# Column sums of the norms on four 32-column tiles of TensorE

## What is computed

```python
def layer_norm(x, g, b):
    mu = xf.mean(-1, keepdims=True)
    var = jnp.square(xf - mu).mean(-1, keepdims=True)
    y = (xf - mu) * lax.rsqrt(var + LN_EPS) * g + b
...
        h = layer_norm(ALPHA * h + mix, ln_mix_g[layer], ln_mix_b[layer])
        ff = conv_ffn(h, ...)
        h = layer_norm(ALPHA * h + ff, ln_ffn_g[layer], ln_ffn_b[layer])
...
def rms_norm(x, g):
    y = xf * lax.rsqrt(jnp.mean(xf * xf, axis=-1, keepdims=True) + EPS)
    return y * g
```

## Time and profile before

| | us |
|---|---|
| median of 3 runs | 1501.68 (1500.94 to 1501.72) |
| profiled execution | 1501.82 |
| its span in the trace | 1500.0 |
| PE busy | 1463.2 (98%) |
| DVE busy | 865.6 (58%) |
| ACT busy | 610.9 (41%) |
| POOL busy | 493.3 (33%) |

### The profile page before, as it was taken

The page is one execution under the profiler, slowest core; times in us unless marked ns, Lnnn a source line. Parts: engine busy times, 40 slices in busy tenths (PEclk is TensorE's granted clock), DMA queues, the critical chain, the costliest instruction groups (busy, mean ns, idle before and its releaser), DMA issues.

```text
span 1500.0 us, 23770 instructions
## 1 busy us (share of the span) xinstructions
PE 1463.2 (98%) x9390; PEld 1207.8 (81%) x9390; DVE 865.6 (58%) x1262; ACT 610.9 (41%) x768; POOL 493.3 (33%) x368
## 2 busy tenths in 40 slices
PE   6999999999999999999999999999999999999999
PEld 5887887898888888889776988888888897777677
DVE  6787777476655660155686667556620374564741
ACT  3655554362223222236565443232221355655541
POOL 3000000215454544532221245545454524422222
PEclk9999999999999999999999999999999999999999
DMA  7421222502223223232202122232223312311211
GB/s 226 116 86 60 83 74 85 183 27 90 109 84 112 84 100 123 85 112 85 85 29 85 57 82 87 88 108 87 109 85 107 130 57 84 132 69 71 71 57 57
DMA packets 22592, 137.24 MB, mean 91 GB/s; under 512 B 2488, under 2 KB 4840, under 8 KB 7280
## 3 DMA queue, kind: packets, MB, share of 16 engines
q1 hardware_dynamic: 17280, 124.79, 23.5%
q10 hardware_dynamic: 5232, 11.32, 2.9%
HBM read 131.89 MB, written 4.21 MB: 91 GB/s over the span
## 4 chain that ended last, share of the span: by engine, by line
issue 41%; PE 27%; POOL 24%; DVE 3%; ACT 2%; DVEq 1%; DMA 1%; ACTq 0%; POOLq 0%; SPq 0%
POOL WL L448 15%; POOL WL L457 9%; PE pair L484 7%; PE pair L486 7%; PE pair L485 7%; PE pair L1079 1%; PE pair L667 1%; ACT WH L1185 1%; PE pair L1066 1%; DVE WL L1672 1%; PE pair L998 1%; PE pair L696 1%; PE pair L1056 1%; DMA RAW<-stream 1%; PE pair L663 0%
## 5 line engine op out<-in xcount | busy, mean ns | idle before, releaser
L484 PE MATMUL pair<-AH,WH 128*128 128x512 f32 (+1 forms) x1240 | 474.7, 383 | 16.8 <-POOL WL L448 12.1
L448 POOL TENSOR_TENSOR WL<-RAW,WH 128x512 fp32r<-128x512 f32 x236 | 321.8, 1396 | 487.6 <-ACT WH L1185 487.6
L486 PE MATMUL pair<-AH,WL 128*128 128x512 f32 (+1 forms) x1240 | 463.5, 374 | 0.0
L485 PE MATMUL pair<-AL,WH 128*128 128x512 f32 (+1 forms) x1240 | 463.3, 374 | 0.0
L1185 ACT ACTIVATE WH<-RAW 128x2048 fp32r<-128x2048 f32 x107 | 204.7, 1913 | 466.1 <-PE pair L486 453.3
L457 POOL TENSOR_TENSOR WL<-RAW,WH 128x512 fp32r<-128x512 f32 x128 | 171.3, 1369 | 500.4 <-ACT WH L1185 500.4
L484 PEld LDWEIGHTS pair<-AH,WH 128*128 128x128 f32 x1240 | 233.6, 188 | 66.2 <-issue 12.4
L486 PEld LDWEIGHTS pair<-AH,WL 128*128 128x128 f32 x1240 | 233.7, 188 | 42.2
L485 PEld LDWEIGHTS pair<-AL,WH 128*128 128x128 f32 x1240 | 233.9, 189 | 41.1 <-issue 1.9
L2015 DVE TENSOR_SCALAR CA<-pair,PAR 128x512 f32<-128x512 f32 x88 | 67.3, 806 | 146.9 <-PE pair L486 144.0
L484 PE MATMUL pair<-GH,WH 128*128 (+2 forms) x416 | 149.8, 360 | 0.1
(11 more groups left out here) (247 smaller groups left out, 1889.2 us busy)
## 6 DMA issues: line engine op xcount, KB each, us to landing
RAW<-stream SPq DMA_DIRECT2D x115, 1024.0 KB, 4.9
H<-x_t SPq DMA_DIRECT2D x3, 1024.0 KB, 9.6
bias_rows<-ROWS ACTq DMA_DIRECT2D x1, 2048.0 KB, 23.0
BIAS<-bias_rows ACTq DMA_DIRECT2D x1, 2048.0 KB, 7.9
FBC<-forget_rows ACTq DMA_DIRECT2D x4, 512.0 KB, 3.6
out<-H ACTq DMA_DIRECT2D x8, 256.0 KB, 2.0
H<-x_t SPq DMA_DIRECT2D x2, 512.0 KB, 6.9
CON<-consts ACTq DMA_DIRECT2D x1, 513.5 KB, 4.2
```

What stands on the lines that cost most here:

```text
L448: pool.tensor_tensor(WL[w][:, part], RAW[raw][:, part], WH[w][:, part].bitcast(F32), ALU.subtract).then_inc(w_lo, 1)
L484: pe.matmul(out_, wh, xh, start=start, stop=False, skip_group_check=shared)
L485: pe.matmul(out_, wh, xl, start=False, stop=False, skip_group_check=shared)
L486: return pe.matmul(out_, wl, xh, start=False, stop=stop, skip_group_check=shared)
```

## The change

Half B's sums of norms 0 to 2 (`tile_sums` in place of `half_sums`): each of the four operands of a sum goes through a 128 x 32 slice of `con["mean"]` into its own 32 output partitions, so the four matmuls use four column tiles of the array. ACT copies the 128 x 256 result out of PSUM into SY3 or SS2 (`take_sums`, put between `square(1, 3)` and `gain(0, 3)`), and PE multiplies that by the whole `con["mean"]` (`tile_totals`, one matmul each, after place 4 of the first chunk). The result is 1/32 of the mean, and `variance` multiplies by 32. The rms sums of both halves go the same way (`rms_tiles`, `take_rms`, `rms_totals`): two rounds of four tiled matmuls, a copy by ACT, one whole matmul. `half_sums` stays for norm 3. `rms_tiles(1)` runs in the middle of `value(1, 0)` and `rms_totals(1)` behind it; before, all of `rms_sums(1)` stood ahead of it. ACT's and DVE's lists of the last norm are put in another order.

```diff
+            def tile_sums(idx):
+                ts = cols_of(1)
+                first, second = (bk(b)[:, ts] for b in LN_SUMS[idx])
+                p = LN_PAIRS[idx][3]
+                pe.wait_ge(y_ready, 8 * idx + 8)
+                pe.wait_ge(y_added, 2 * idx + 2)
+                for g, y in enumerate((SY3[:, 1, 0], SY3[:, 1, 1], H[:, 2 * p, ts], H[:, 2 * p + 1, ts])):
+                    mm = pe.matmul(first[BLK * g:BLK * g + BLK], con["mean"][:, 0:BLK], y, start=True, stop=True)
+                mm.then_inc(t_summed, 1)
+                pe.wait_ge(y2_added, 2 * idx + 2)
+                pe.wait_ge(y_squared, 8 * idx + 8)
+                for g, y2 in enumerate((SS2[:, 1, 0], SS2[:, 1, 1], SQ2[:, 1, 3, 0], SQ2[:, 1, 3, 1])):
+                    mm = pe.matmul(second[BLK * g:BLK * g + BLK], con["mean"][:, 0:BLK], y2, start=True, stop=True)
+                mm.then_inc(t_summed, 1)
+            def tile_totals(idx):
+                for power, tiles in enumerate((SY3, SS2)):
+                    pe.wait_ge(t_copied, 2 * idx + power + 1)
+                    pe.matmul(bk(LN_SUMS[idx][power])[:, cols_of(1)], con["mean"], tiles[:, 1, 0], start=True, stop=True).then_inc(y_summed, 1)
...
-                half_sums(idx)
+                tile_sums(idx)
...
-                part(c0, 0, range(4, 8))
+                part(c0, 0, (4,))
+                tile_totals(idx)
+                part(c0, 0, (5, 6, 7))
...
-            def rms_sums(half):
+            def rms_tiles(half):
                 ts = cols_of(half)
-                for i, p in enumerate(LN_PAIRS[3]):
-                    pe.wait_ge(h_squared, 4 * half + i + 1)
-                    for c in range(2):
-                        mm = pe.matmul(bk(6 + half)[:, ts], con["mean"], SQ2[:, half, i, c], start=i == 0 and c == 0, stop=i == 3 and c == 1)
-                mm.then_inc(h_summed, 1)
+                for r in range(2):
+                    pe.wait_ge(h_squared, 4 * half + 2 * r + 2)
+                    for g in range(4):
+                        mm = pe.matmul(bk(6 + half)[BLK * g:BLK * g + BLK, ts], con["mean"][:, 0:BLK], SQ2[:, half, 2 * r + g // 2, g % 2],
+                                       start=r == 0, stop=r == 1)
+                mm.then_inc(h_tiled, 1)
+            def rms_totals(half):
+                pe.wait_ge(h_copied, half + 1)
+                pe.matmul(bk(6 + half)[:, cols_of(half)], con["mean"], SQ2[:, half, 0, 0], start=True, stop=True).then_inc(h_summed, 1)
...
-            rms_sums(0)
+            rms_tiles(0)
+            rms_totals(0)
...
-            rms_sums(1)
-            value(1, 0)
+            value(1, 0, mid=lambda: rms_tiles(1))
+            rms_totals(1)
...
+                def take_sums():
+                    for power, tiles in enumerate((SY3, SS2)):
+                        act.wait_ge(t_summed, 2 * idx + power + 1)
+                        act.activation(tiles[:, 1, 0], bk(LN_SUMS[idx][power])[:, cols_of(1)], ACT.Copy).then_inc(t_copied, 1)
+                def take_rms(half):
+                    act.wait_ge(h_tiled, half + 1)
+                    act.activation(SQ2[:, half, 0, 0], bk(6 + half)[:, cols_of(half)], ACT.Copy).then_inc(h_copied, 1)
...
                     last_gain(0, 3)
+                    take_rms(0)
+                    spread(1)
+                    last_spread(0)
                     split_early(c0 + 2)
...
-                    spread(1)
-                    last_spread(0)
-                    last_gain(1, 0)
                     high(0, 0)
                     high(0, 1)
+                    last_gain(1, 0)
+                    split_next(c0 + 1)
                     last_gain(1, 1)
                     last_gain(1, 2)
-                    split_next(c0 + 1)
+                    high(0, 2)
                     last_gain(1, 3)
-                    high(0, 2)
                     high(0, 3)
+                    take_rms(1)
...
+                take_sums()
                 gain(0, 3)
...
-                    dve.tensor_copy(MEAN[:, ts], mean)
+                    if half and idx < 3:
+                        dve.tensor_scalar(MEAN[:, ts], mean, float(BLK), None, ALU.mult)
+                    else:
+                        dve.tensor_copy(MEAN[:, ts], mean)
...
                     centre(1, 1)
+                    scale(1, 1)
                     last_low(0, 0)
-                    scale(1, 1)
                     last_low(0, 1)
                     centre(1, 2)
                     scale(1, 2)
+                    gained(0, 2)
                     centre(1, 3)
                     scale(1, 3)
-                    gained(0, 2)
                     gained(0, 3)
```

More of the change, by code:

```diff
@@ L278, in build @@
         sg_made, pool_w_loaded, sink_put = sem("sg_made"), sem("pool_w_loaded"), sem("sink_put")
+        t_summed, t_copied, h_tiled, h_copied = (sem(n) for n in ("t_summed", "t_copied", "h_tiled", "h_copied"))
         z_abs, z_exp, f_made, f_stored = (sem(n) for n in ("z_abs", "z_exp", "f_made", "f_stored"))
@@ L1023, in gates, with value @@
                 half(E_CHUNK[j], m)
-            def value(part, t):
+            def value(part, t, mid=None):
                 n = N_V + part
@@ L1029, in value @@
                 for k in range(4):
+                    if mid and k == 2:
+                        mid()
                     if t == 0:
@@ L1364, in last_spread @@
                     act.wait_ge(h_summed, half + 1)
-                    rstd(VAR[:, ts], bk(6 + half)[:, ts], 1.0, con["eps_rms"]).then_inc(h_rstd, 1)
+                    rstd(VAR[:, ts], bk(6 + half)[:, ts], float(BLK), con["eps_rms"]).then_inc(h_rstd, 1)
                 def high(half, p):
@@ L1890, in variance @@
                     dve.wait_ge(y_summed, 4 * idx + 2 * half + 2)
-                    dve.tensor_tensor(VAR[:, ts], second, VAR[:, ts], ALU.subtract)
+                    if half and idx < 3:
+                        dve.scalar_tensor_tensor(VAR[:, ts], second, float(BLK), VAR[:, ts], ALU.mult, ALU.subtract)
+                    else:
+                        dve.tensor_tensor(VAR[:, ts], second, VAR[:, ts], ALU.subtract)
                     dve.drain()
```

## The result

The changed kernel takes 1514.02 us (median of 6 runs, 1512.93 to 1515.14) against 1500.79 us (6 runs of the kernel before beside it): ratio 1.0086, 95% interval 1.0075 to 1.0097. It is slower by 13.2 us; 1508.6 was forecast, with 1511.5 as the upper end. The direction was right; about half of the loss was seen coming. The profiled execution took 1512.93 us, its span 1511.1.

What follows compares the result with a forecast made beforehand. PE and half B's chain were taken to end together, so delaying gain(0,3) costs time: norms 0 to 2 +7.3, last norm -0.4, sum +6.9 us on 1501.82, giving a median of 1508.6 us, range 1504.0 to 1511.5.

Steps and rivals of the forecast that it cites:

- What bounds the norms: Norms 0 to 2: PE and half B's chain end together; the chain hangs on gain(0,3), delayed by 2.45 us.
- What the change takes off PE: Sums: 1.64 us less in each of three norms, 2.05 us less twice for the rms sums, together 9.0 us.
- Rival (2): All tiled sums: the tiles run one by one, each norm losing 1.23 us more; 1514 us; chance 5%.
- Norms 0 to 2, +7.3: Half B of three norms: ACT's copies delay gain(0,3), losing 2.45, 2.4 and 2.45 us, in sum +7.3 us.
- Nothing later takes it back: Behind norms 0 to 2: PE has no such idle time and ACT's next weight split moves along; +7.3 us stays.
- The last norm, -0.4: Last norm: of 4.1 us taken off PE, 0.4 us is left after stalls; bounds -2.9 and +1.5.
- The same step, second place: Last norm: last_spread(1), behind copy, VM and the head's inverse root on ACT, comes at 1251.0, not 1250.64.
- The sum: Whole kernel: 7.3 - 0.4 = +6.9 us on 1501.82, so 1508.7; as a median 1508.6 us.
- The range: Whole kernel: 1504.0 to 1511.5 us, meant to hold 8 in 10.
- Rivals (1): Whole kernel: PE's saved time reaches the end, the rms halves giving 4.1 us; 1497.7 us; chance 6%.
- Rival (3): Whole kernel: the delay is real but half is made up by slack or shorter stalls; 1503 us; chance 7%.

Runs made afterwards that it cites:

- e3: The changed kernel with only take_sums moved behind gain(0,3) on ScalarE: 1509.63 us.
- e6: The kernel before with only the last norm's new order of ScalarE and VectorE, no tiles or copies: 1506.39 us.
- e4: The changed kernel with only the last norm's split_next(c0+1) moved back behind last_gain(1,2) on ScalarE: 1511.75 us.
- e5: The kernel before plus the last norm's change, with split_next(c0+1) behind last_gain(1,2), rms_tiles(1) ahead of value(1,0), rms_totals(1) in its middle: 1502.57 us.
- e8: The changed kernel with useless matmuls in PE's waits, three ahead of each half B of norms 0 to 2, twelve ahead of value(1,0): 1512.71 us.
- e1: The changed kernel with the whole last norm as before, so only half B's sums of norms 0 to 2 are tiled: 1508.8 us.

## Why the prediction was right in direction and wrong in size

- **What bounds the norms** (PE and half B's chain end together, and the chain hangs on gain(0,3)): right. gain(0,3) was put at 315.40 and came at 315.42, half B at 324.30 and came at 324.28; e3 shows the place of the copies to be the cause. That it is right to 0.02 us is luck: ACT's second copy came 0.1 us later than worked out, and the gain followed on it 0.1 us sooner.
- **What the change takes off PE**: right in the main. The tiles run side by side: the two rounds and the copy brought the first total to 1236.85 - 5.55 = 1231.30, where 1231.3 had been worked out. A round took 0.57 us from start to next start (311.82 to 312.39) for 0.48, and by norm 0 and the first rms sum I estimate 8 us off PE for 9.0. The busy time fell by only 4.1, in part because matmuls at half clock take longer. Rival (2), that the tiles run one by one, is out; that its 1514 is the measured time is chance.
- **Norms 0 to 2, +7.3**: 8.2 came. Norms 1 and 2 cost 2.24 and 1.91 for 2.4 and 2.45; norm 0 cost 4.03. The term that was missing is the clock behind PE's wait, 1.6 us. The wait was in the working and the clock in the earlier trace rows, and the one was never asked what it does to the other. Slices of 37 us that all show 9 are no evidence for stretches of 3 us, nor for what a wait would do that the kernel before does not have.
- **"Nothing later takes it back"**: right; the differences stand still between norms.
- **The last norm, -0.4**: +5.5 came. This is the step that failed, in two places. First, AL(0,2) was put "near 1246.2" and came at 1255.37 + 0.69 - 5.55 = 1250.5. It was DVE and not ACT that made it late: high(0,2) came at 1246.7. POOL's hold-ups had only been given as a bound, from the one lengthened row. But the new list brings the second split forward, POOL has eight subtractions in a row, and most of DVE's instructions beside them took about 1 us longer each. The order without tiles costs 4.62, of which some 1.7 are the clock (e6), and putting the split back takes 2.9 us off (e4).
- **The same step, second place**: ACT's list was taken as the bound of last_spread(1), 1251.0. It came at 1263.28 - 5.55 = 1257.7, since the tiles stand on PE behind the wait for AL(0,2), and the total behind the rest of value(1,0). The stall had been named, but not what is queued behind it. With the split back and the tiles first the last norm is at +0.40 (e5). The slow clock has a share here too, about 2.1 us by e8, from one profile.
- **The sum**: 7.3 - 0.4 = +6.9 forecast, 8.2 + 5.5 = 13.7 in the profiles. Of the 6.8 between them 5.9 are the last norm, 1.6 are norm 0's clock, and norms 1 and 2 took 0.7 less.
- **The range**: its bound for the last norm, +1.5, took one hold-up for all of them. Eight instructions of POOL that can each add about 1 us to one of DVE's would have been the bound, and the range would have held the time.
- **Rivals (1) and (3)**: both out. PE's saved work reached the end nowhere, and no norm made up half of its delay. (Rival (3)'s 1503 did not follow from its own words either: half of 7.3 us made up leaves 1505.)

## What to carry to other kernels

An engine that is busy 98% can still have nothing to give: where the chain that it waits for ends just as it arrives, work taken off it turns into waiting. If the saving is paid for with an instruction on the engine that carries the chain, that instruction costs what it waits for and not its length (here 2.4 us for a copy of 0.38 us). And a list that moves a GpSimd job has to be priced by how many VectorE instructions fall beside it (here about 1 us each).

## What the hardware showed that was not expected

After PE had waited 1.9 us in norm 0, and 5.3 us in the last norm, it was granted 0.50 (1.2 GHz) for 3 us and more, though it had work all along. Waits of 1.7 us in norms 1 and 2 of the same execution were followed by 1.00, and so were the waits filled with useless matmuls. The length of the last wait does not decide it: 1.74 us in norm 0 of e1 and e4 were followed by half clock, and 2.88 us in e5 by 1.00 throughout. What does was not found. The Trainium skill (TensorE: Matmul & The Clock Gate, Part 1: The HAM clock gate) describes a gate that lowers TensorE's clock after idle time; the traces here agree that the fall follows on idle time and that filled waits don't bring it, but not that every such wait brings it.

A lower clock is also seen ahead of all changed code, in some profiles and not in others. The stretch from 52 to 60 us of the profile, first the kernel before, then the changed one:

```profile
52.00:60.00 8.00, 8.00 (x64) 5.95 (x64) 7.03 (x12) 3.46 (x3) 0.00 (x0) 0.79 0.39 133
```

```profile
52.00:60.00 8.00, 8.00 (x76) 6.28 (x74) 7.73 (x11) 2.86 (x2) 0.00 (x0) 1.00 0.40 133
```

The clock is 0.79 against 1.00, with 64 matmul records against 76. This is part of the -2.61 at the start of the changed kernel's shifts, and why the spans of two profiles (1500.0 and 1511.1) differ by 2.6 us less than what the change did.

Where DVE had one instruction after another beside running subtractions of POOL, its 128x512 ones took 1.62 to 1.78 us for 0.69, about as long as one of POOL's. An instruction that came by itself was held up by less: the two lows of e4 beside POOL's second four took 1.34 and 0.82 us. The Trainium skill (SBUF — State Buffer, Terms) describes a port pair that the two engines share under an exclusive lock, held for a whole instruction while the other is blocked; the traces agree, since the first has to wait for one subtraction each time and the second only for the rest of one. POOL is held up as well: its subtractions, some 1.42 us each in the kernel before (5.66 / 4), took 1.67 (6.66 / 4 in e4) where DVE had work beside all of them.
